# A fused two-block transformer kernel: sixteen modulation blocks loaded at once, and half of their sum given to TensorE

## The reference

```python
c_act = jax.nn.silu(c)
cond = c_act @ ada_w[i] + ada_b[i]          # ada_w: 1024 x 6144
shift1, scale1, gate1, shift2, scale2, gate2 = jnp.split(cond, N_MOD, axis=-1)
# rmsnorm: x * rsqrt(mean(x * x, axis=-1) + EPS) * g;  modulate: h * (1 + scale) + shift
h = modulate(rmsnorm(x, norm1_g[i]), shift1, scale1)
z = h @ w_in[i] + b_in[i]                   # w_in: 1024 x 2048
...
```

## Time and profile before

| | |
|---|---|
| three runs | 1757.25, 1761.7, 1760.7 us (median 1760.7) |
| span of the profiled execution, first to last instruction | 1757.1 us |
| TensorE matmul busy | 1679.6 us, 96% |
| VectorE, ScalarE, GpSimd busy | 916.1, 627.2, 225.3 us |
| mean granted clock of TensorE | 0.983 of full speed |

### The profile page before, as it was taken

The page is one execution under the profiler, slowest core; times in us unless marked ns, Lnnn a source line. Parts: engine busy times, 40 slices in busy tenths (PEclk is TensorE's granted clock), DMA queues, the critical chain, the costliest instruction groups (busy, mean ns, idle before and its releaser), DMA issues.

```text
span 1757.1 us, 22185 instructions
## 1 busy us (share of the span) xinstructions
PE 1679.6 (96%) x8263; PEld 1311.8 (75%) x8263; DVE 916.1 (52%) x1376; ACT 627.2 (36%) x946; POOL 225.3 (13%) x204
## 2 busy tenths in 40 slices
PE   1999899999999999999999999999998999999996
PEld 1757688888888867666667788888887688888885
DVE  6765676544334463666667544444336644444223
ACT  1324334222223362554555333333226333333221
POOL 5010106998000030000000000003000000000000
PEclk9999999999999999999998999999999899999998
DMA  7565134454332241111101322233211133333221
GB/s 281 204 200 167 40 110 161 169 181 157 109 107 97 69 117 64 37 37 49 37 25 61 108 96 95 95 100 115 98 57 49 61 98 100 99 96 115 92 80 48
DMA packets 48588, 179.27 MB, mean 102 GB/s; under 512 B 5968, under 2 KB 6640, under 8 KB 48272
## 3 DMA queue, kind: packets, MB, share of 16 engines
q1 hardware_dynamic: 43600, 162.04, 27.5%
q0 software_dynamic: 3776, 14.78, 2.7%
q10 hardware_dynamic: 1152, 1.66, 0.4%
HBM read 173.04 MB, written 2.10 MB: 100 GB/s over the span
## 4 chain that ended last, share of the span: by engine, by line
PE 71%; issue 22%; DVE 5%; DMA 1%; ACT 1%; ACTq 1%; POOL 0%; POOLq 0%; DVEq 0%; SPq 0%
PE bank L383 15%; PE bank L385 14%; PE bank L384 14%; PE bank L1437 3%; PE bank L1439 2%; PE bank L1438 2%; PE bank L1545 2%; PE bank L1501 2%; PE bank L1521 2%; DVE ada_acc L1972 1%; PE bank L1172 1%; PE bank L1174 1%; PE bank L1173 1%; PE bank L454 1%; PE bank L1394 1%
## 5 line engine op out<-in xcount | busy, mean ns | idle before, releaser
L309 DVE TENSOR_TENSOR w_lo<-raw,w_hi 128x1024 fp32r<-128x1024 f32 (+1 forms) x229 | 316.4, 1382 | 575.2 <-ACT w_hi L305 574.9
L305 ACT ACTIVATE w_hi<-raw 128x1024 fp32r<-128x1024 f32 (+1 forms) x229 | 258.0, 1127 | 564.4 <-PE bank L385 482.7
L383 PE MATMUL bank<-h_hi,w_hi 128*128 128x512 f32 x1136 | 448.0, 394 | 0.5 <-DVE w_lo L309 0.5
L385 PE MATMUL bank<-h_hi,w_lo 128*128 128x512 f32 x1136 | 442.2, 389 | 0.0
L384 PE MATMUL bank<-h_lo,w_hi 128*128 128x512 f32 x1136 | 442.2, 389 | 0.0
L383 PEld LDWEIGHTS bank<-h_hi,w_hi 128*128 128x128 f32 x1136 | 213.2, 188 | 50.2 <-issue 5.2
L385 PEld LDWEIGHTS bank<-h_hi,w_lo 128*128 128x128 f32 x1136 | 213.2, 188 | 45.0
L384 PEld LDWEIGHTS bank<-h_lo,w_hi 128*128 128x128 f32 x1136 | 213.3, 188 | 44.6 <-issue 1.7
L383 PE MATMUL bank<-hid_hi,w_hi 128*128 128x512 f32 x528 | 205.6, 389 | 0.0
L384 PE MATMUL bank<-hid_lo,w_hi 128*128 128x512 f32 x528 | 205.4, 389 | 0.0
L385 PE MATMUL bank<-hid_hi,w_lo 128*128 128x512 f32 x528 | 205.4, 389 | 0.0
(11 more groups left out here) (397 smaller groups left out, 2079.5 us busy)
## 6 DMA issues: line engine op xcount, KB each, us to landing
raw<-in_f2i SPq DMA_DIRECT2D x88, 512.0 KB, 3.3
raw<-in_ffi SPq DMA_DIRECT2D x44, 512.0 KB, 3.4
raw<-in_f2o SPq DMA_DIRECT2D x32, 704.0 KB, 4.0
ada_w<-in_ada_w SPq DMA_DIRECT2D x24, 512.0 KB, 4.3
m_out<-in_ada_w POOLq DMA_DIRECT2D x24, 512.0 KB, 3.7
raw<-in_att_w SPq DMA_DIRECT2D x23, 512.0 KB, 3.3
raw<-in_ffo SPq DMA_DIRECT2D x16, 704.0 KB, 4.0
raw<-in_ada_w SPq DMA_DIRECT2D x16, 512.0 KB, 4.9
```

Source lines behind the costliest of these rows:

```text
L305: nc.scalar.activation(WH[par][:, 0:kc * P], RAW[s][:, 0:kc * P], ACT.Copy).then_inc(whi, count)
L309: nc.vector.tensor_tensor(WL[par][:, 0:kc * P], RAW[s][:, 0:kc * P], WH[par][:, 0:kc * P].bitcast(F32), ALU.subtract).then_inc(wlo, count)
L383: pe_.matmul(bank[:, :], w_h, hi[:, k0 + k, :], start=start and k == 0, stop=False)
L385: last = pe_.matmul(bank[:, :], w_l, hi[:, k0 + k, :], start=False, stop=stop and k == kc - 1)
```

## The change

- SyncE issues fifteen of the sixteen modulation blocks without waiting for VectorE, a scale block and a shift block in turn, into sixteen places: scale blocks 0 to 3 in `RAW`, 4 to 7 in a new tile `head_blocks`, shift blocks in `h_scratch`, `v_tok` and `conv`. X comes behind three of them.
- VectorE multiplies and adds scale blocks 0 to 6. Scale block 7 and the eight shift blocks go to TensorE, which multiplies them directly: eight matmuls a block with 128 columns of the block as the stationary operand and one column of `c_act` as the moving one.
- TensorE sums the squares of X from the eight chunks themselves (32 one-column matmuls), and GpSimd's running sum is gone. GpSimd's tiles of conv weights (L1034) are now made after the last normed chunk.
- VectorE multiplies X by the token scale, in place over the squares, before the modulation is there. Behind the modulation ScalarE makes the high part straight from that (scale and shift in one instruction), VectorE the same value in `TMP` and from it the low part.
- Two semaphores of a later stage are merged with others that are free by then.

The diff, cut to its core:

```diff
@@ sync
-            for s in range(4):
-                load(s, ada_w[s], D)
+            scale_block(0)
+            scale_block(1)
+            shift_block(0)
             sp.dma_start(X[:, :, :], xT).then_inc(ld_x, 16)
-            with sp.Fori(1, 4) as r:
-                for s in range(4):
-                    sp.wait_ge(raw_used, 4 * (r - 1) + s + 1)
-                    load(s, ada_block(4 * r + s), D)
+            for k in range(2, C - 1):
+                scale_block(k)
+                shift_block(k - 1)
+            shift_block(C - 2)
+            sp.wait_ge(raw_used, 1)
+            load(0, w_in[0], D)
+            scale_block(C - 1)
+            shift_block(C - 1)
...
@@ gpsimd
-            pool_sum(nj["n1"], C, sq_p1)
             pool_rsqrt(nj["n1"])
+            pool.wait_ge(n_lo, nj["n1"].lo + C)
@@ tensor
+            def squares_summed(nj_):
+
                 for k in range(C):
+                    pe_.wait_ge(n_sq, nj_.sq + k + 1)
+                    for i in range(TC):
+                        m = pe_.matmul(NS[:, i:i + 1], sq_p1(k)[:, i * P:(i + 1) * P], ONE[:, 0:1],
+                                       start=k == 0 and i == 0, stop=k == C - 1 and i == TC - 1, skip_group_check=True)
+                m.then_inc(n_used, 1)
+
+            def shift_columns(k):
+
+                if k < C - 2:
+                    pe_.wait_ge(ld_shift[k // 2], 32)
+                else:
+                    pe_.wait_ge(ld_shift[k - 3], 16)
+                for c in range(C):
+                    m = pe_.matmul(PS[5][:, c:c + 1], SHIFT_AT[k][:, c * P:(c + 1) * P], CACT[:, k:k + 1],
+                                   start=k == 0 and c == 0, stop=k == C - 1 and c == C - 1, skip_group_check=True)
+                return m
+
+            def scale_columns():
+
+                pe_.wait_ge(raw_used, C - 1)
+                for c in range(C):
+                    pe_.matmul(PS[4][:, c:c + 1], AAC[:, 1, c * P:(c + 1) * P], ONE[:, 0:1], start=c == 0, stop=False,
+                               skip_group_check=True)
+                pe_.wait_ge(ld_scale[C - 1], 16)
+                for c in range(C):
+                    m = pe_.matmul(PS[4][:, c:c + 1], SCALE_AT[C - 1][:, c * P:(c + 1) * P], CACT[:, C - 1:C],
+                                   start=False, stop=c == C - 1, skip_group_check=True)
                 m.then_inc(ada_sum, 1)
...
-            pe_sum(nj["n1"])
-            ada_sums(0, PS[5], raw_used, C)
-            pe_bcast(nj["n1"])
-            ada_sums(1, PS[5], raw_used, 2 * C)
+            pe_.wait_ge(c_ready, 1)
+            shift_columns(0)
+            squares_summed(nj["n1"])
+            for k in range(1, C - 1):
+                shift_columns(k)
+                if k == C - 4:
+                    pe_bcast(nj["n1"])
+            scale_columns()
+            shift_columns(C - 1).then_inc(ada_sum, 1)
@@ scalar
-            split_hi(1, 1, 1, C, R_P1, first=True)
-            act_parts(nj["n1"], C, shift=lambda k: MOD[:, k:k + 1])
+            act.wait_ge(mod_ready, 3)
+            for k in range(C):
+                act.wait_ge(n_t, nj["n1"].t + k + 1)
+                act.activation(HH[:, k, :], sq_p1(k), ACT.Identity, bias=MOD[:, k:k + 1],
+                               scale=GS[:, 0, k:k + 1]).then_inc(n_hi, 1)
+                if k == 0:
+                    split_hi(1, 1, 1, C, R_P1, first=True)
@@ vector
+                if k == C - 5:
+                    dve_mean(nj["n1"], D)
+                if k == C - 4:
                     dve.wait_ge(const_ready, 1)
-                    dve_diag(nj["n1"], D)
+                    dve_diag(nj["n1"], D, mean=False)
+
+            def x_by_token(k):
+                dve.tensor_tensor(sq_p1(k), X[:, k, :], RB[:, :], ALU.mult).then_inc(n_t, 1)
+
+            dve.wait_ge(n_rb, nj["n1"].turn)
+            for k in range(C - 2):
+                x_by_token(k)
             split_lo(0, 0, 0, C)
...
+            for k in range(C):
+                if k >= 2:
+                    dve.wait_ge(n_lo, nj["n1"].lo + k - 1)
+                dve.tensor_scalar(TMP[:, k % 2, :], sq_p1(k), GS[:, 0, k:k + 1], MOD[:, k:k + 1], ALU.mult,
+                                  ALU.add).then_inc(n_t, 1)
+                if k >= 1:
+                    first_low(k - 1)
+                if k == 2:
+                    split_lo(1, 1, 1, C)
+            first_low(C - 1)
```

More of the change, by code:

```diff
@@ L60 @@
 ADA_C = ADA_L * C
-R_P1 = ADA_A // 4
+R_P1 = 1
 G = {"w_out": 2, "ffi0": 11, "ffo0": 4, "att5": 2, "att6": 4, "att_out": 2, "ffi1": 11, "ffo1": 4,
@@ L91, in build_program @@
             PWG = sub.enter_context(nc.sbuf_tensor("pool_w_gained", [P, 4, S], F32))
+        with ExitStack() as sub:
+            HB = sub.enter_context(nc.sbuf_tensor("head_blocks", [P, 4, D], F32))
         HH = sb("h_hi", [P, C, S], F32R)
@@ L147, in build_program, with two @@
             R8 = SIG[0:GB, :]
+            def two(tile, i):
+                return tile[:, 2 * i:2 * i + 2, :].rearrange("p a s -> p (a s)")
+            SCALE_AT = [RAW[i][:, 0:D] for i in range(4)] + [HB[:, i, :] for i in range(4)]
+            SHIFT_AT = [two(HS, i) for i in range(4)] + [two(VT, 0), two(VT, 1), two(CV, 0), two(CV, 1)]
         with ExitStack() as life:
@@ L242, in build_program @@
         ld_late = [sem(f"late_ada_loaded{i}") for i in range(2)]
+        ld_scale = ld + ld_ada
+        ld_shift = [sem(f"shift_pair_loaded{i}") for i in range(3)] + [
+            sem(f"shift_block_loaded{k}") for k in (C - 2, C - 1)]
         late_mul, late_used = sem("late_ada_multiplied"), sem("late_ada_added")
@@ L277, in build_program @@
         f_hi, f_lo, f_sh = sem("final_lead_hi_ready"), sem("final_lead_lo_ready"), sem("final_shift_halves_ready")
-        f_step, f_bias, f_rq, f_lx, f_ng = (sem("final_lead_" + k) for k in ("step", "bias", "scaled", "forget", "gates"))
+        f_step, f_lx, f_ng = (sem("final_lead_" + k) for k in ("step", "forget", "gates"))
         class Norm:
@@ L879, in load, with scale_block, shift_block @@
                 sp.dma_start(RAW[s][:, 0:width], src).then_inc(ld[s], 16)
-            def ada_block(i):
-                return ada_w[bass.ds(i, 1), :, :].rearrange("a p n -> (a p) n")
-            for s in range(4):
-                load(s, ada_w[s], D)
-            sp.dma_start(X[:, :, :], xT).then_inc(ld_x, 16)
-            with sp.Fori(1, 4) as r:
-                for s in range(4):
-                    sp.wait_ge(raw_used, 4 * (r - 1) + s + 1)
-                    load(s, ada_block(4 * r + s), D)
+            def scale_block(k):
+                sp.dma_start(SCALE_AT[k], ada_w[C + k]).then_inc(ld_scale[k], 16)
+            def shift_block(k):
+                sp.dma_start(SHIFT_AT[k], ada_w[k]).then_inc(ld_shift[k // 2 if k < C - 2 else k - 3], 16)
+            scale_block(0)
+            scale_block(1)
+            shift_block(0)
+            sp.dma_start(X[:, :, :], xT).then_inc(ld_x, 16)
+            for k in range(2, C - 1):
[6 more added lines that the diff above has]
+            shift_block(C - 1)
+            sp.wait_ge(raw_used, 2)
+            load(1, w_in[1], D)
+            sp.wait_ge(raw_used, 3)
+            load(2, w_in[2], D)
+            sp.wait_ge(raw_used, 4)
+            load(3, w_in[3], D)
             def load_ada(i, src):
                 sp.dma_start(AWB[:, i % 4, :], src).then_inc(ld_ada[i % 4], 16)
[L896 to L899, removed]
+            for i in range(4):
+                if i < 3:
+                    sp.wait_ge(raw_used, 5 + i)
+                else:
+                    sp.wait_ge(ada_sum, 1)
+                load_ada(i, ada_w[ADA_A + i])
             def shifted(c):
@@ L1986, in _, with first_low @@
             gain(0, 8, "norm1").then_inc(mod_ready, 1)
+            dve.wait_ge(ada_sum, 2)
+            dve.tensor_tensor(MOD[:, 0:8], PS[5][:, 0:C], VEC[:, COL["ada_b"]:COL["ada_b"] + C], ALU.add).then_inc(mod_ready, 1)
             dve.wait_ge(mod_ready, 3)
-            dve_parts(nj["n1"], C, lambda k: X[:, k, :], lambda k: GS[:, 0, k:k + 1], shift=lambda k: MOD[:, k:k + 1],
-                      between=lambda k: split_lo(1, 1, 1, C) if k == 1 else None)
+            dve.wait_ge(n_t, nj["n1"].t + C)
+            def first_low(k):
+                dve.wait_ge(n_t, nj["n1"].t + C + k + 1)
+                dve.wait_ge(n_hi, nj["n1"].hi + k + 1)
+                dve.tensor_tensor(HL[:, k, :], TMP[:, k % 2, :], HH[:, k, :].bitcast(F32), ALU.subtract).then_inc(n_lo, 1)
+            for k in range(C):
[8 more added lines that the diff above has]
+            first_low(C - 1)
             def ada_add(i):
                 j, k = divmod(i, C)
-                dve.wait_ge(ld_ada[i % 4], 16 * (i // 4 + 1))
+                dve.wait_ge(ld_ada[i % 4], 16 * (i // 4 + 2))
                 if i:
```

41 lines of the change are left out of this document (18 added, 23 removed).

## The result

| | before | changed |
|---|---|---|
| runs, median | 1759.45 us (4 runs, 1757.25 to 1761.7) | 1780.49 us (4 runs, 1775.26 to 1781.63) |
| span of the profiled execution | 1757.1 us | 1773.5 us |
| ratio of the runs | | 1.0115, 95% interval 1.0098 to 1.0132 |

The changed kernel is slower by about 20 us (1.15% of 1759.45), between 17 and 23 by the interval. Its profiled execution is its fastest run; the device's time of that run is 1775.26, 1.8 us above the span. Wherever a run of this case lists both, the time is 1.7 to 1.9 us above the span; the 0.15 us named for the kernel before compares two different executions.

A forecast was written before the change was run, and what follows sets the result against it. The start of TensorE's dense products was taken to bound the kernel: +19.1 us for the head, -0.8 behind the modulation, +18.3 on 1757.1 gives 1775.4; with 3.6 to the median 1779, said 1778, range 1770 to 1785.

The forecast's parts named there:

- the sum: Whole kernel: +19.1 us in the head less 0.8 behind the modulation, +18.3 on the profiled span of 1757.1: 1775.4.
- the step from span to median: Whole kernel: the median of the runs lies 3.6 us above the profiled execution.
- The stream: TensorE in the head: 224 one-column instructions at 0.213 us, 47.8 us at the lower clock level, ending at 66.3 us.
- The first landing: Head, loads: TensorE starts when the first pair of shift blocks is there, at 16.5 us; X comes at 14.0.
- VectorE's cover: Head: VectorE's work lies hidden under TensorE's stream; it waits some 15 us for the squares' sum, 9 for the broadcast.
- Behind the modulation: From the modulation to the products: first product after 1.95 us, chunk 2 after some 6.0, 0.8 us earlier than now.
- the clock in the first products: First dense products: point at which they get the upper clock level taken as now, +-1.5 us.
- A: Rival, TensorE's stream in the head: the clock rises in it, -8.7 us, 1752; chance 0.07, another 0.05 for a later rise.
- B: Rival, head: nineteen outstanding transfers slow the first pair or TensorE stalls, 2 to 6 us, 1780 to 1786; chance 0.13.
- C: Rival, head: the scale's arrival, not TensorE, sets the start; within 1 us of now, 1760; chance 0.02.
- shorter multiply-adds: VectorE in the head: without GpSimd's seven additions its seven multiply-adds take 1.29 us each, not 2.11.
- something that comes later: GpSimd's conv weight tiles wait for the last low half, about 80 us; first use at about 106; counted at nothing.

The follow-up runs named there:

- pool_sum: The changed kernel with the squares summed on GpSimd again and four one-column matmuls instead of 32 on TensorE: span 1765.1 us.
- dense_ahead: The changed kernel with seven 128x512 fp32 matmuls of ones ahead of the first shift block: span 1773.2 us.
- bcast_early: The changed kernel with the broadcast of the token scale behind the second shift block instead of the fifth: span 1777.7 us.
- dense_between: The changed kernel with six 128x512 fp32 matmuls of ones ahead and fourteen more in the stream, one per 16 instructions: span 1794.8 us.
- all_dve: The changed kernel with all sixteen blocks on VectorE again and normed chunks as before the change: median 1751.04 us, ratio to before 0.9947.

## Why the prediction was right

The time fell in the range, 2.5 us from the number, and the mechanism is the one named. That the number is as near as that is in part luck: in the profiled execution the sum is 1.9 us too high, while the step from span to median, taken as 3.6 us, was 7.0 (1780.49 less 1773.5). Of the 3.6, 1.8 lie between span and time of any run, and the rest is one draw from the spread below. By its own steps:

- **The stream.** 224 instructions at 0.213 us from 16.5 us, end at 66.3: measured from 16.35 to 66.0. No one-column matmul of the head was at the upper level. pool_sum took 56 away and got 11.5 us for them; dense_ahead showed that even a stream that starts at the upper level loses it. This was the whole sign of the result.
- **The first landing.** 16.5 us, from equal bytes ahead in the queue: 16.35, and 16.11 to 17.38 in the five other profiles with that order. X was used at 13.67, said 14.0. The queue ran at 403 to 417 GB/s.
- **VectorE's cover.** Said to wait some 15 and 9 us: 14.8 and 9.9. bcast_early took the second wait away and gained nothing.
- **Behind the modulation.** First product 2.0 us after the stream's end, said 1.95. The tensor_scalar of 512 columns takes 0.54 us, taken 0.4 with bounds 0.38 and 0.75. Third chunk 71.72, said 72.3.
- **Mis-sized: the clock in the first products.** It was carried over from before (upper level 4 us after the third chunk's start) with +-1.5 us. In the eleven profiles it came up between 2.4 and 9.0 us after the first product, and each microsecond at the lower level costs about half of one. In the profiled execution it was up at the third chunk's start; this gave back 1.9 of the 17.7 us by which that chunk was late, and the span grew by 16.4 against the sum's 18.3. In the second profile of the changed kernel it came up 5.3 us behind that start and gave nothing back.
- **Left out: executions of one kernel differ by 2 to 8 us.** Two sources show in the profiles, the moment of the rise and the stretches of lower clock around 130 to 200 us. The median difference of 21 us compares other executions than the profiled pair; 1777.1 less 1757.1 is 20.0, 1773.5 less 1760.3 is 13.2. The interval of the ratio, 17 to 23 us, holds the sum's 18.3.
- **Rivals.** A (clock rises in the stream): excluded by the trace, dense_ahead and dense_between. B (worse load): the measured 1780.49 would have suited it too, so only the trace decides, and there it has nothing: the first start is 16.35, the queue kept its pace, and TensorE worked without a gap in the stream. (From 1778, 2 to 6 us more are 1780 to 1784, not 1786.) C (stream hidden): excluded by the chain. Its "23 us before TensorE comes to it" is a slip, by the prediction's own times some 16; measured 39.2 and 55.6 us. The advice of the Trainium skill, TensorE: Matmul & The Clock Gate, section on why this matters for your kernels, to keep TensorE busy did not carry over to this work: it was busy for 50 us at 1.2 GHz.

What the prediction did not ask is whether the other parts alone are a gain. They are: all_dve keeps the loads, the squares on TensorE and the later conv weight tiles, leaves out the nine blocks on TensorE and the new way to the normed chunks, and is some 9 us faster than the kernel before; moving the nine blocks gave that away, with 20 more. By the rows most of the 9 us is VectorE freed from GpSimd, from the squares (5.0) and the conv weight tiles (some 3.4 by the estimate above), and little of it the loads into sixteen places. The prediction had the first of these as shorter multiply-adds; the tiles it had only as something that comes later.

## What to carry to other kernels

A matmul of one moving column is not a cheap one: each brings a load of 128 stationary columns with it (333 ns, and PEld is as full as PE in the stream), and here at the lower clock eight of them for one 512 KB block took 3.41 us of TensorE, where VectorE multiplies and adds the same block in 1.28. Price the work in the form that it will have on the idle engine before moving it there. When a change has a part that takes work off an engine and a part that puts it on another, time the two apart: here they had opposite signs.

## What else the runs showed of the hardware

- Dense work raises the clock, but doesn't keep it up for one-column work: in dense_ahead the fall came some 3 us into the stream (granted 0.79 at 18 to 20 us), and in dense_between one 128x512 matmul among sixteen one-column instructions left it at 0.50 from 18 to 62 us. The clock column shows the lower level in the head only once there has been a rise and a fall; before that it reads 1.00, and only the durations (352 ns, or 250) tell.
- SyncE's issue of a 512 KB transfer takes 0.4 to 0.7 us until X and eleven blocks are issued; the next took 3.29 us, and the three after it about 1 or less, one later 2.88 (timeline of SyncE in the changed kernel):

```profile
7.22 0.44 SPq L896 DMA_DIRECT2D v_tok<-in_ada_w  x1
7.71 3.29 SPq L893 DMA_DIRECT2D head_blocks<-in_ada_w  x1
11.04 1.02 SPq L896 DMA_DIRECT2D v_tok<-in_ada_w  x1
12.11 1.03 SPq L896 DMA_DIRECT2D conv<-in_ada_w  x1
```

It may be that the queue takes no more until some of its work is done; no run tried this by itself, so it is not shown.
